# Second block's joints: norm chain and first tile by halves of the tokens, scaled outputs in PSUM, a weight chunk's high part by VectorE, other squares summed inside the last group

## What is computed

```python
def _rms(x, g):
    xf = x.astype(jnp.float32)
    y = xf * lax.rsqrt(jnp.mean(xf * xf, axis=-1, keepdims=True) + EPS)
    return (y * g.astype(jnp.float32)).astype(x.dtype)

for i in range(DEPTH_2):
    g = norm_g[i]
    hn = _rms(x, g[0])
    ...                                  # m = conv, pool or attention mixer of hn
    x = x + _rms(m, g[1])
    f = _swiglu(_rms(x, g[2]), ffn_w_gate[i], ffn_w_up[i], ffn_w_down[i])
    x = x + _rms(f, g[3])
return x
```

## Time and profile before

| | us |
|---|---|
| median of 3 runs | 2790.94 (2790.88 to 2792.4) |
| the profiled execution | 2790.47 |
| its span, first to last instruction | 2788.7 |
| outside the span in it | 1.77 |

### The profile page before, as it was taken

How to read it: one execution, slowest core, us unless ns; L and a number is a source line. 1 busy time by engine, 2 the same in 40 slices (tenths; PEclk the granted TensorE clock), 3 DMA queues, 4 the chain that set the end, 5 groups by cost and what they waited for, 6 DMA issues and landing times.

```text
span 2788.7 us, 37052 instructions
## 1 busy us (share of the span) xinstructions
PE 2747.2 (99%) x13804; PEld 2280.7 (82%) x13804; DVE 1327.2 (48%) x1825; ACT 938.9 (34%) x1318; POOL 1235.3 (44%) x913
## 2 busy tenths in 40 slices
PE   9999999999999999999999999999999999999997
PEld 6888877887888888888888888878888888888886
DVE  3444675668455441175441276565441174544413
ACT  4443446743133222252222334342222321422222
POOL 3444442134535555515555443235454454454554
PEclk9999999999999999999999999999999999999999
DMA  8556231122323333313333321223333332233333
GB/s 311 166 194 192 73 124 54 32 61 76 98 76 106 95 97 101 112 68 113 91 97 106 98 89 59 61 61 113 98 98 101 103 91 91 83 105 98 91 106 98
DMA packets 106251, 285.09 MB, mean 102 GB/s; under 512 B 38733, under 2 KB 38861, under 8 KB 104851
## 3 DMA queue, kind: packets, MB, share of 16 engines
q1 hardware_dynamic: 99488, 258.33, 30.8%
q10 hardware_dynamic: 6643, 25.05, 2.6%
HBM read 281.08 MB, written 8.85 MB: 104 GB/s over the span
## 4 chain that ended last, share of the span: by engine, by line
issue 41%; PE 34%; POOL 23%; DVE 1%; POOLq 0%; ACT 0%; DMA 0%; ACTq 0%
POOL w_lo L646 23%; PE ps L450 11%; PE ps L452 11%; PE ps L451 11%; PE ps L514 0%; DVE x L2557 0%; DVE tmp L2551 0%; POOLq L644 0%; PE ps L503 0%; POOLq L166 0%; PE ps L731 0%; PE ps L753 0%; DMA par<-in_cols 0%; PE ps L531 0%; PE ps L498 0%
## 5 line engine op out<-in xcount | busy, mean ns | idle before, releaser
L646 POOL TENSOR_TENSOR w_lo<-w_raw,w_hi 128x512 fp32r<-128x512 f32 x904 | 1234.4, 1389 | 1542.6 <-ACT w_hi L443 1542.6
L450 PE MATMUL ps<-u_hi,w_hi 128*128 128x512 f32 x2256 | 885.1, 392 | 9.6 <-DVE u_lo L2300 6.5
L452 PE MATMUL ps<-u_hi,w_lo 128*128 128x512 f32 x2256 | 878.2, 389 | 0.0
L451 PE MATMUL ps<-u_lo,w_hi 128*128 128x512 f32 x2256 | 878.0, 389 | 0.0
L443 ACT ACTIVATE w_hi<-w_raw 128x1024 fp32r<-128x1024 f32 x452 | 475.3, 1055 | 784.0 <-PE ps L452 739.8
L450 PEld LDWEIGHTS ps<-u_hi,w_hi 128*128 128x128 f32 x2256 | 423.5, 188 | 104.4 <-DVE u_lo L2300 10.7
L452 PEld LDWEIGHTS ps<-u_hi,w_lo 128*128 128x128 f32 x2256 | 423.5, 188 | 88.8
L451 PEld LDWEIGHTS ps<-u_lo,w_hi 128*128 128x128 f32 x2256 | 423.6, 188 | 88.3 <-issue 1.9
L450 PE MATMUL ps<-h_hi,w_hi 128*128 128x512 f32 (+1 forms) x726 | 277.9, 383 | 0.0
L452 PE MATMUL ps<-h_hi,w_lo 128*128 128x512 f32 (+1 forms) x726 | 277.8, 383 | 0.0
L451 PE MATMUL ps<-h_lo,w_hi 128*128 128x512 f32 (+1 forms) x726 | 277.7, 383 | 0.0
(11 more groups left out here) (342 smaller groups left out, 3008.8 us busy)
## 6 DMA issues: line engine op xcount, KB each, us to landing
w_raw<-in_stream SPq DMA_DIRECT2D x452, 512.0 KB, 3.6
late_ring<-in_ada_late ACTq DMA_DIRECT2D x32, 512.0 KB, 5.6
ada_ring<-in_ada SPq DMA_DIRECT2D x8, 1024.0 KB, 17.5
dilated_bias_rows<-dilated_bias SPq DMA_DIRECT2D x18, 244.1 KB, 4.9
band_a<-dilated_bias_rows SPq DMA_DIRECT2D x96, 28.0 KB, 2.0
x<-in_x SPq DMA_DIRECT2D x8, 256.0 KB, 17.2
bias_rows<-bias_scratch ACTq DMA_DIRECT2D x4, 512.0 KB, 7.7
out_yT<-x SPq DMA_DIRECT2D x8, 256.0 KB, 2.0
```

The source lines that it names most:

```text
L450: nc.tensor.matmul(o, w[0], v[0], start=start, stop=False)
L451: nc.tensor.matmul(o, w[0], v[1], start=False, stop=False)
L452: return nc.tensor.matmul(o, w[1], v[0], start=False, stop=stop)
L646: ins = nc.gpsimd.tensor_tensor(w_lo[:, s, half], w_raw[:, s, half], w_hi[:, s, half].bitcast(F32), ALU.subtract)
```

## The change

At five joints (conv 0 to up 0, down 1 to attention, attention to up 2, down 2 to conv 1, conv 1 to up 3):

- The four sums of `acc` (`sums_at`) move from behind the last group into it, ahead of its seventh product of 8 (conv and attention outputs) or its seventeenth of 22 (down). They go to banks 7 and 5.
- The last output's square, its sums, the root, the reciprocal and the spread are each done for tokens 0 to 255 and then for 256 to 511, the factors in banks 6 and 7. Of `keep_busy`, one matmul stands ahead of the spread instead of two, and four behind it instead of six.
- VectorE no longer copies the last output to `y`; ScalarE does, behind the second root. VectorE makes the high part of the missing weight chunk in its place (`last_output`), and ScalarE no longer does.

At these five and at the pool layer's joint (which keeps one root, one reciprocal and one spread):

- `scaled_y` writes to PSUM, banks 4 and 5 in turn, instead of `tmp`, and the addition reads it there.
- Tile 0 is scaled, added, rounded and multiplied for the first 256 tokens and then for the others (`first_tile_halves`): 24 matmuls of 256 columns in place of 12 of 512.

The joint from down 0 to the pool layer and the end of the program keep their steps. The down stage of layers 1 and 2 is written out on TensorE, as it was for layer 3, instead of a loop of two rounds.

```diff
+FIRST, SECOND = slice(0, S // 2), slice(S // 2, S)
+HALVES = (FIRST, SECOND)
+SUM_BANKS = (7, 5)
...
+    def pe_factor_halves(pe, n):
+
+        for half in range(2):
+            pe.wait_ge(y_last_sq, n.up("last"))
+            for r in (2 * half, 2 * half + 1):
+                mm = pe.matmul(bank(SUM_BANKS[half], P, at=r * P), sq[:, 1, r * P:(r + 1) * P], ones[:, :],
+                               start=False, stop=r == 2 * half + 1)
+            mm.then_inc(y_sums, 1)
+        keep_busy(pe, 6, 1, 2 * P)
+        for half in range(2):
+            pe.wait_ge(y_factor, n.up("fin"))
+            for b in (2 * half, 2 * half + 1):
+                mm = pe.matmul(bank(6 + half, P, at=b % 2 * P), bass.AP(col, 12 + b, [[32, P], [0, P]]), ident[:, :],
+                               start=True, stop=True)
+            mm.then_inc(y_spread, 1)
+        keep_busy(pe, 0, 4, 2 * P)
...
-        keep_busy(pe, 5, 6, 2 * P)
+        keep_busy(pe, 7, 6, 2 * P)
...
+            def sums_at(step):
+
+                def before(k):
+                    if k == step:
+                        pe.wait_ge(acc_ready, n.up("acc"))
+                        for r in range(QB):
+                            pe.matmul(bank(SUM_BANKS[r // 2], P, at=r * P), acc[:, r * P:(r + 1) * P], ones[:, :],
+                                      start=r % 2 == 0, stop=False)
+                return before
+
+            def first_tile_halves(c0):
+
+                for half, w in enumerate(HALVES):
+                    if half:
+                        pe.wait_ge(u_ready, n["u"] - KD + 1)
+                    else:
+                        pe.wait_ge(u_half, n.up("uh"))
+                    for j in range(4):
+                        if half == 0:
+                            pe.wait_ge(lo_ready, c0 + j + 1)
+                        product(bank(j, 2 * P, at=2 * P * half), chunk_tiles((c0 + j) % RING, 0),
+                                (u_hi[:, 0, w], u_lo[:, 0, w]), half == 0, False)
+
...
+                if halves:
+                    first_tile_halves(c0)
+                for k in range(1 if halves else 0, KD - late):
...
+                              sums_at(16) if layer in (1, 2) and it == 1 and j == 3 else None)
...
-            def scaled_parts(layer, which, windows_at=None):
...
+                    if halves and t == 0:
+                        w = SECOND
+                        act.wait_ge(x_half, n.up("xh"))
+                        nc.scalar.activation(u_hi[:, t, FIRST], x[:, t, FIRST], ACT.Copy,
+                                             scale=par[:, g0:g0 + 1]).then_inc(u_hi_half, 1)
...
+            def half_squares(used, b):
+
+                act.wait_ge(chunk_used, used)
+                act.wait_ge(sq_used, n["squ"] - 1)
+                for w in HALVES:
+                    nc.scalar.activation(sq[:, 1, w], ps[:, b, w], ACT.Square).then_inc(y_last_sq, 1)
+
+            def half_root(half, b=None):
+
+                act.wait_ge(y_sums, n.up("last"))
+                c = 2 * half
+                nc.scalar.activation(col[:, 12 + c:14 + c], summed(SUM_BANKS[half] if b is None else b)[:, c:c + 2], ACT.Sqrt, bias=eps_rms[:, 0:1],
+                                     scale=1.0 / D).then_inc(dev_ready, 1)
+
+            def finish_halves(nxt, stage, b):
+
+                n.up("out", KD)
+                half_root(0)
+                half_root(1)
+                nc.scalar.activation(y[:, KD - 1, :], bank(b), ACT.Copy).then_inc(out_evac, 1)
+                begun.add(stage)
+                scaled_parts(*nxt, halves=True)
+                act.wait_ge(hi_ready, BASE[stage] + RING)
 
             def last_square(used, b):
...
+            def first_half_tile(layer, which):
+
+                dve.wait_ge(u_hi_half, n.up("u_hi_half"))
+                g0 = norm_col(layer, which, 0)
+                nc.vector.scalar_tensor_tensor(out=u_lo[:, 0, FIRST], in0=x[:, 0, FIRST], scalar=par[:, g0:g0 + 1],
+                                               in1=u_hi[:, 0, FIRST].bitcast(F32), op0=ALU.mult,
+                                               op1=ALU.subtract).then_inc(u_half, 1)
...
+            def last_output(stage, used):
+
+                c = BASE[stage] + RING - 1
+                slot = c % RING
+                dve.wait_ge(landed[slot], 16 * (c // RING + 1))
+                dve.wait_ge(chunk_used, used)
+                dve.wait_ge(hi_ready, c)
+                nc.vector.tensor_copy(w_hi[:, slot, :], w_raw[:, slot, :]).then_inc(hi_ready, 1)
+                n.up("out")
+                n.up("last", 2)
+
+            def finish_halves(layer, which, nxt, factor_halves=True):
+
+                for half in range(2 if factor_halves else 1):
+                    c = col[:, 12 + 2 * half:14 + 2 * half] if factor_halves else col[:, 12:12 + QB]
+                    dve.wait_ge(dev_ready, n.up("dev"))
+                    nc.vector.reciprocal(c, c).then_inc(y_factor, 1)
+
+                factor = ps[:, 6:8, 0:S // 2] if factor_halves else ps[:, 6, :].rearrange("p (h e) -> p h e", h=2)
+
+                def scaled_y(t, h=slice(0, 2)):
+
+                    g0 = norm_col(layer, which, t)
+                    ch.later(nc.vector.scalar_tensor_tensor(out=ps[:, 4 + t % 2, :].rearrange("p (h e) -> p h e", h=2)[:, h],
+                                                            in0=y[:, t, :].rearrange("p (h e) -> p h e", h=2)[:, h],
+                                                            scalar=par[:, g0:g0 + 1], in1=factor[:, h], op0=ALU.mult,
+                                                            op1=ALU.mult))
+
+                def add_y(t, done, w=slice(0, S)):
+
+                    ch.sync()
+                    nc.vector.tensor_tensor(x[:, t, w], x[:, t, w], ps[:, 4 + t % 2, w], ALU.add).then_inc(done, 1)
+
+                dve.wait_ge(y_spread, n.up("fin"))
+                scaled_y(0, slice(0, 1))
+                add_y(0, x_half, FIRST)
+                if factor_halves:
+                    dve.wait_ge(y_spread, n.up("fin"))
+                scaled_y(0, slice(1, 2))
+                dve.wait_ge(out_evac, n["out"])
+                first_half_tile(nxt[0], nxt[1])
+                for t in range(KD):
+                    add_y(t, x_done, slice(0, S) if t else SECOND)
+                    if t + 1 < KD:
+                        scaled_y(t + 1)
+                    next_parts(nxt, t + 1, slice(0, S) if t else SECOND)
...
```

More of the change, by code:

```diff
@@ L1121, in out8 @@
                         pe.wait_ge(out_evac, count0 + m - 3)
-                    group(pe, bank(m % 4), base + m, 0, [(0, k, m_parts(k)) for k in range(KD)])
+                    group(pe, bank(m % 4), base + m, 0, [(0, k, m_parts(k)) for k in range(KD)],
+                          before=in_last if m == KD - 1 else None)
                     if m == 2 and after_third:
@@ L1453, in _ @@
                 else:
-                    group(pe, bank(C_OUT_BANKS[m]), BASE["c_out"] + m, 0, [(0, k, m_parts(k)) for k in range(KD)])
-            pe_factor(pe, n)
+                    group(pe, bank(C_OUT_BANKS[m]), BASE["c_out"] + m, 0, [(0, k, m_parts(k)) for k in range(KD)],
+                          before=sums_at(6) if m == KD - 1 else None)
+            pe_factor_halves(pe, n)
             ffn(2)
@@ L2605, in conv @@
                 ch(nc.vector.memset(acc[:, :], 0.0))
[L2606 removed]
+                for m in range(KD - 1):
                     dve.wait_ge(chunk_used, BASE[f"conv_out{which}"] + m + 1)
                     evac_y(m, m % 4)
[L2609 to L2611 removed]
+                last_output(stage, BASE[f"conv_out{which}"] + KD)
+                finish_halves(layer, 1, nxt)
+            conv(0, 0, (0, 2, True), "up0")
             ffn(0, (1, 0, False))
```

95 lines of the change are left out of this document (52 added, 43 removed).

## The result

The changed kernel takes 2795.38 us (median of 22 runs, 2793.9 to 2796.98); the kernel before took 2790.91 (22 runs, 2788.12 to 2792.55). The ratio is 1.0016, 95% interval 1.001 to 1.0023: 4.5 us slower, where 1.6 faster was forecast, and above the range, which ended at 2792.8. In short: the chain through each joint ran as planned, but at the end of each changed opening one VectorE addition fell behind a GpSimd instruction, took 1.67 us instead of 0.69, and TensorE waited for it.

A forecast was written before the change was run, and what follows sets the result against it. TensorE, busy 99% of the span, was taken as the bound. Five joints gaining 1.29 - 1.00 each, plus 0.17 at the pool layer's joint, sum to 1.6 us: 2789.3 us, range 2786.5 to 2792.8.

The forecast's parts named there:

- The sums in the group: Sums of acc moved inside the last group, where nothing hides them: +1.00 us per joint (0.90 to 1.10), five joints.
- The chain in halves: Square to first opening matmul, in 256-token halves: first matmul 4.6 us behind the group's end, 2.1 earlier than before.
- The outputs in PSUM: Scaled outputs written to PSUM and added from there: 0 us, bounds -0.01 and +0.06 per addition.
- VectorE's cast: High part of the missing weight chunk made on VectorE: some 0.7 us at 1024 columns, costing 0.
- TensorE stops at tile 1: After both half tiles TensorE waits 0.6 us for tile 1's `u_lo`, leaving 0.29 gained per joint.
- the pool's joint: Joint out of the pool layer, where no sums move: 0.17 us gained.
- The rest of the opening: From tile 1 to the sum of squares of x: VectorE's lead shrinks from 0.64 to 0.07 us, no wait.
- the first: Rival: additions from PSUM are slower, at 0.065 each the sum of squares waits 0.5 us; 2792.3 us; chance 0.19.
- The second: Rival: TensorE does not stop at tile 1, gaining 5.8 us in all; 2785.1 us; chance 0.06.
- the third: Rival: the halves cost 0.3 us more in the chain and nothing is gained; 2790.9 us; chance 0.17.
- The fourth: Rival: the clock falls to 1.2 GHz in part of five joints' openings, costing 15 us; 2805 us; chance 0.03.

The follow-up runs named there:

- the first experiment: Changed kernel with the last square of x written to PSUM bank 4 at the six changed joints; 2788.84 us, ratio 0.9991.
- the last run: Kernel before with one edit, the last square of x written to a free PSUM bank at every joint; 2789.94 us, ratio 0.9999.

## Why the prediction was wrong

**The sums in the group**: forecast 1.00, measured 0.82 (813.72 to 814.54) and 0.08 at the successor (0.31 instead of 0.227), 0.90. The term was 0.10 too large, at the edge of its bounds.

**The chain in halves**: first scaling at E'+2.54 (818.69), forecast 2.55. ScalarE's high part for 256 columns 0.51, estimated 0.50. First half tile at E'+4.67, forecast 4.6. Low part of tile 1 done at 824.30, E'+8.15, forecast 8.11; its matmuls at 8.21, with the standing start 8.32, forecast 8.28. Every step held.

**The outputs in PSUM**: forecast 0, measured 0.68 for the addition and 0.75 for the scaling that writes PSUM, as from SBUF; in time, nothing. The rule of the Trainium skill that the prediction set against it ("Perfetto Trace Analysis", "Optimizing Scalar/DVE Operations": some 60 ns of access for SBUF, 125 for PSUM) would have given additions of about 0.75; no row here shows it. **VectorE's cast** took 0.69 (816.24), forecast 0.7, and cost nothing. **TensorE stops at tile 1**, as said, by 0.39 to 0.42 (0.25 at the pool's joint), not 0.6.

**The step that failed** is in "The rest of the opening": "the margin is used up to the last hundredth; I take no wait". The shrinking of the margin was worked out rightly (TensorE 1.29 earlier, VectorE 0.72), but the last addition was given the 0.69 that it had before, as if its length went with it. Its neighbour in time was not looked at. In the trace of before GpSimd started 0.20 behind it, and GpSimd's start goes with TensorE's. A shift of 0.57 between TensorE and VectorE (0.45 between GpSimd and VectorE as measured) had to cross 0.20. The measured wait is 0.71 to 0.74 at each of six joints. The prediction had its price in its own rows (1.46 instead of 0.42 beside GpSimd), used it for the half addition of the first tile, and did not ask it of the five additions at the end of the opening. One more line of the list of waits would have told as well: the wait of 1.0 at the layer-norm joint is this very collision, in the kernel before.

Where that addition is safe, the forecast is the result: the first experiment's stretches sum to -1.67 against -1.6 forecast, and its median is 2788.84 against 2789.3. Part of that agreement is luck: the pool's joint (up 1) gained 0.04 instead of 0.17, the stretch of up 2 gained 0.45 instead of 0.29, and 0.4 outside the span was not in the forecast at all, which took the 1.77 of the kernel before. The wait costs 0.88 to 0.98 at five joints (changed less last square in PSUM, by column) and 0.47 at up 2, 5.1 in all. The stretch of up 2 holds the attention of c_in. TensorE's first score product there, before and in the changed kernel:

```profile
1631.54 0.47 PE L450 MATMUL ps<-kc_hi,qc_hi 128*128 128x512 f32 x1 [1.58 <-issue]
```

```profile
1634.49 0.47 PE L457 MATMUL ps<-kc_hi,qc_hi 128*128 128x512 f32 x1 [0.79 <-issue]
```

The idle time ahead of it is 0.79 shorter in the changed kernel (and 0.58 shorter than the 1.37 of the first experiment), so part of a delay is taken back there. The joints' 3.44 is 1.0 short of the 4.5 between the medians. Of this 0.4 is outside the span and 0.14 behind the last of the points. The rest lies within what single executions of one kernel spread by.

**The rivals**: the first forecast a loss at the right place, the sum of squares, by the wrong cause. Both it and the true one rest on the used-up margin; its own size, 2792.3, is 3.1 short. The second is out, for TensorE did stop at tile 1, and so is the third: the chain came within 0.1 of what was laid out. The fourth is out too: no changed joint lost clock in the profile, where the granted clock is 1.00 from 642 to the end of the last opening.

**What the prediction did not ask**: whether the move into the group was worth having. It priced it at 1.00 against 0.05 behind the group, since there it lay under the square. With the square in halves less lies under it, but still enough: the sums behind the group cost 0.15 at tile 1.

## What to carry to other kernels

When a change moves one engine against another, list for each instruction whose length depends on company which neighbour starts within the shift, before and after: an order of 0.2 us decided a wait of 0.7 us here, six times over. A wait of the same kind elsewhere in the list is a free measurement of what it costs. Work that is put into a busy engine's stretch to take it off a chain should first be tried behind it, under whatever is left there.

## What the runs showed of the hardware

The long addition has a rule in these runs: an addition of SBUF operands into SBUF that starts while GpSimd's SBUF subtraction is at work ends a fixed time after that one instruction of GpSimd ends. (In the trace of the kernel before, 128 of VectorE's TENSOR_TENSOR instructions of 128x512 with both inputs in SBUF start inside one of GpSimd's subtractions into `w_lo`, at least 0.15 ahead of its end. Each ends 0.54 to 0.56 behind it. Another 58 with an input in PSUM start so, and each takes 0.68 or 0.69.) In the changed kernel GpSimd ends at 842.29 (840.91 + 1.38) and the addition at 842.83, 0.54 later. In the kernel before with the late addition it is 840.30 and 840.85, 0.55. With the sums behind the group, where GpSimd's instruction runs from 841.51 for 1.42 and the addition from 841.80 for 1.67, it is 0.54. For 256 columns it is 0.28 in the kernel before: GpSimd's instruction there takes 1.30 from 2766.14, the addition ends at 2767.72:

```profile
2766.14 1.30 POOL L646 TENSOR_TENSOR w_lo<-w_raw,w_hi 128x512 fp32r<-128x512 f32 x1 [7.88 <-ACT w_hi L443]
```

and 0.28 in the run with the outputs in SBUF (815.23, 815.51), where it cost nothing: 0.28 behind the end of GpSimd is just where a start at 815.09 with 0.42 ends anyway. It reads as if such an addition did not begin its work until GpSimd's instruction was through, 0.54 being its 0.69 less some 0.15 at its start; the inside of it is inferred. An addition already under way when GpSimd starts is not held (839.45 before, 657.07 in the last run), and one with an operand in PSUM is not held at all (838.71 in the first experiment).

It holds the other way as well. GpSimd's instruction takes 1.30 with VectorE out of the way; behind an addition that got there first it is 1.65 in the kernel before (839.65 to 841.30) and 1.52 with the first tile whole (840.44 to 841.96), which is 1.16 and 1.15 behind the end of that addition (840.14 and 840.81). So whichever starts first goes through and the other is held until then. With the addition's operand in PSUM GpSimd is not held either: 1.29 in the last run. The changed kernel's own 1.38 fits: GpSimd starts at 840.91 in the middle of the last addition but one (840.44 to 841.13) and ends 1.16 behind it, and the last addition, which starts at 841.16, finds GpSimd ahead of it.

The Trainium skill, "SBUF — State Buffer", "SBUF: two separate sides", has this: the port pair that VectorE and GpSimd share is "an exclusive lock, not a bandwidth split", taken for a whole instruction by whichever starts first, and VectorE needs it, against a GpSimd instruction that reads SBUF, for an instruction with two SBUF inputs. The traces agree in each of these points, as far as lengths can show it: held until about the other's end (0.54 and 1.16 behind it), both ways round, and free with one operand in PSUM. The prediction had not applied it to this addition.
